# A hybrid decoder step: the state-space scan's states stored by step within the chunk, chunks innermost

## What is computed

```python
a = rmsnorm(h); z = a @ w_in               # q, k, v, o, gates and u
hm = mlstm_chunkwise(q, k, v, ig, lf, ...) # 4 heads of 256
bu = einsum('gpc,bsgc->bsgp', Bb, u)       # complex: bu_re, bu_im; 64 groups x 64 states, 16 channels each
bu[:, 0] += ab * s0                        # the state before, complex
st = associative_scan(st[t] = ab * st[t-1] + bu[t])      # complex, over the tokens
ys = einsum('gcp,bsgp->bsgc', C_re, st_re) - einsum(..., C_im, st_im) + Dd * u
ys = gelu(ys); ys = ys * sigmoid(ys @ w_glu + b_glu)
h = h + concat(hm, ys) @ w_out
h = h + peer_ffn(rmsnorm(h)); h = h + (p @ w_ple_proj) * sigmoid(rmsnorm(h) @ w_ple_gate)
```

## Time and profile before

| | us |
|---|---|
| median of 3 runs | 3019.16 |
| lowest, highest run | 3017.88, 3020.06 |
| span of the profiled execution, first to last instruction (its own time beside the span is not listed) | 3016.9 |
| TensorE busy in it | 2834.0 (94%) |
| VectorE busy | 1717.4 (57%) |
| ScalarE busy | 1213.0 (40%) |

### The profile page before, as it was taken

How to read it: one execution, slowest core, us unless ns; L and a number is a source line. 1 busy time by engine, 2 the same in 40 slices (tenths; PEclk the granted TensorE clock), 3 DMA queues, 4 the chain that set the end, 5 groups by cost and what they waited for, 6 DMA issues and landing times.

```text
span 3016.9 us, 53624 instructions
## 1 busy us (share of the span) xinstructions
PE 2834.0 (94%) x19564; PEld 2661.5 (88%) x19564; DVE 1717.4 (57%) x3311; ACT 1213.0 (40%) x2023; POOL 2.5 (0%) x18
## 2 busy tenths in 40 slices
PE   8999946899899998799999999999999999999997
PEld 6677734669799997699999999999999999999887
DVE  2289895566658887933333333335555555555466
ACT  1200002213344446944444444444444444444443
POOL 0000000000000000000000000000000000000000
PEclk9799977779899999999999999999999999999999
DMA  6124412226543331033333333344445544444543
GB/s 163 56 91 132 139 56 86 87 84 182 157 133 125 125 129 66 0 125 127 137 125 126 136 127 125 132 151 166 166 167 167 164 155 162 162 166 166 171 112 115
DMA packets 218075, 389.29 MB, mean 129 GB/s; under 512 B 21348, under 2 KB 167396, under 8 KB 200676
## 3 DMA queue, kind: packets, MB, share of 16 engines
q1 hardware_dynamic: 218020, 388.56, 39.0%
HBM read 374.04 MB, written 14.49 MB: 129 GB/s over the span
## 4 chain that ended last, share of the span: by engine, by line
PE 78%; DVE 14%; issue 4%; ACT 2%; DVEq 1%; DMA 0%; ACTq 0%
PE ps L389 11%; PE ps L390 11%; PE ps L391 11%; PE ps L1182 9%; PE ps L1185 9%; PE ps L1181 9%; PE ps L1113 7%; PE ps L261 3%; PE ps L812 1%; PE ps L1723 1%; DVE work L544 1%; DVE work L547 1%; DVE work L539 1%; DVE work L540 1%; DVE work L541 1%
## 5 line engine op out<-in xcount | busy, mean ns | idle before, releaser
L389 PE MATMUL ps<-ffn_h,part_h 128*128 128x288 f32 x2176 | 685.8, 315 | 14.8 <-issue 10.3
L390 PE MATMUL ps<-ffn_l,part_h 128*128 128x288 f32 x2176 | 642.3, 295 | 0.0
L391 PE MATMUL ps<-ffn_h,part_l 128*128 128x288 f32 x2176 | 639.1, 294 | 0.0
L1181 PE MATMUL ps<-act_h,v_high 128*128 128x288 f32 x2048 | 551.8, 295 | 6.1 <-DVE act_l L1418 3.6
L1182 PE MATMUL ps<-act_l,v_high 128*128 128x288 f32 x2048 | 552.2, 295 | 0.0
L1421 DVE TENSOR_TENSOR v_low<-ring,v_high 128x1024 fp32r<-128x1024 f32 x256 | 313.8, 1226 | 372.1 <-ACT v_high L1292 372.1
L1214 ACT CAST part_h<-ps 128x512 fp32r<-128x512 f32 x512 | 299.7, 586 | 466.1 <-PE ps L1113 465.4
L445 DVE TENSOR_TENSOR part_l<-ps,part_h 128x512 fp32r<-128x512 f32 x368 | 254.0, 691 | 404.9 <-ACT part_h L1214 402.4
L389 PEld LDWEIGHTS ps<-ffn_h,part_h 128*128 128x128 f32 x2176 | 409.8, 188 | 18.0 <-issue 16.2
L390 PEld LDWEIGHTS ps<-ffn_l,part_h 128*128 128x128 f32 x2176 | 412.0, 189 | 0.0
L391 PEld LDWEIGHTS ps<-ffn_h,part_l 128*128 128x128 f32 x2176 | 409.7, 188 | 0.0
(11 more groups left out here) (339 smaller groups left out, 3212.2 us busy)
## 6 DMA issues: line engine op xcount, KB each, us to landing
ring<-in_peer_u SPq DMA_DIRECT2D x128, 1024.0 KB, 5.3
ring<-in_peer_v SPq DMA_DIRECT2D x128, 1024.0 KB, 5.6
ring<-in_w_in SPq DMA_DIRECT2D x20, 2048.0 KB, 8.0
ring<-in_w_out SPq DMA_DIRECT2D x16, 1024.0 KB, 5.9
ring<-in_w_ple_gate SPq DMA_DIRECT2D x16, 1024.0 KB, 5.9
out<-work SPq DMA_DIRECT2D x37, 256.0 KB, 3.2
work<-in_state_mlstm_C SPq DMA_DIRECT2D x32, 256.0 KB, 4.9
ring<-in_peer_w_q SPq DMA_DIRECT2D x8, 1024.0 KB, 5.7
```

Source lines behind the costliest of these rows:

```text
L389: pe.matmul(bank, w_h, rhs_h, start=start, stop=False)
L390: pe.matmul(bank, w_h, rhs_l, start=False, stop=False)
L391: return pe.matmul(bank, w_l, rhs_h, start=False, stop=stop)
L1181: pe.matmul(ps[c][:, 0:T], w_h, a_h, start=st_, stop=False)
```

## The change

The states get two arrays for each part: `stp` for the prompt, indexed step, tile, chunk, and `sts` for the samples, indexed step, tile, request. What one step of the scan touches is then one dense piece: 512 elements for the prompt, 256 for the samples. The copies out of PSUM put the states in that order: each of the 2 x 32 copies becomes two instructions, one over 256 and one over 32 elements, that read PSUM with a step between neighbours. TensorE's y matmuls read the states from the two arrays, so each becomes two, of 256 and 32 columns, and their result is in the order of the arrays; VectorE's operation on it puts the tokens back in order, again in two instructions. The bytes, the arithmetic and the buffers' places are the same.

```diff
--- before.py
+++ after.py
@@ -176,11 +176,16 @@
                 ap = ap.rearrange("p (a b c) -> p a b c", b=shape[1], c=shape[2])
             return ap
 
+        def by_step(ap, n):
+
+            return ap.rearrange("p (c s) -> p s c", s=n)
+
         def bc(ap, n):
 
             return ap.unsqueeze(len(ap.shape)).to_broadcast([*ap.shape, n])
 
-        st = [wk(O_RE, NJ, T), wk(O_IM, NJ, T)]
+        stp = [wk(o, CH, NJ, NCH) for o in (O_RE, O_IM)]
+        sts = [wk(o + NJ * TP, NS, NJ, NB) for o in (O_RE, O_IM)]
         zT = wk(O_Z, 32, T)
         uT = wk(O_U, 8, T)
         mix = wk(O_MIX, 16, T)
@@ -572,22 +577,20 @@
             for _ in range(3):
                 cmul(v, o, pw, pw, pw, ts)
 
-            smp = [s[:, :, TP:T].rearrange("p j (b s) -> p s j b", s=NS) for s in st]
             s0 = [s0T[:, q, :].rearrange("p (b j) -> p j b", j=NJ) for q in range(2)]
             aB = [bc(x, NB) for x in a]
             for s in range(NS):
-                src = s0 if s == 0 else [x[:, s - 1] for x in smp]
-                cmul_add(v, o, [x[:, s] for x in smp], aB, src, [t[:, :, 0:NB] for t in tS])
-
-            chk = [s[:, :, 0:TP].rearrange("p j (k t) -> p t j k", t=CH) for s in st]
+                src = s0 if s == 0 else [x[:, s - 1] for x in sts]
+                cmul_add(v, o, [x[:, s] for x in sts], aB, src, [t[:, :, 0:NB] for t in tS])
+
             aC = [bc(x, NCH).unsqueeze(1) for x in a]
             tC = [t.unsqueeze(1) for t in tS]
             with v.Fori(0, CH - 1) as i:
                 o.loop(i, {"dve_own": CMUL})
-                cmul_add(v, o, [x[:, ds(i + 1, 1)] for x in chk], aC, [x[:, ds(i, 1)] for x in chk], tC)
+                cmul_add(v, o, [x[:, ds(i + 1, 1)] for x in stp], aC, [x[:, ds(i, 1)] for x in stp], tC)
                 o.leave(CH - 1)
 
-            end = [s[:, :, CH - 1:TP:CH] for s in st]
+            end = [x[:, CH - 1] for x in stp]
             with v.Fori(0, NCH - 1) as i:
                 o.loop(i, {"dve_own": CMUL})
                 cmul_add(v, o, [x[:, :, ds(i + 1, 1)] for x in end], [x.unsqueeze(2) for x in pw],
@@ -601,14 +604,14 @@
             prev = [x[:, :, 0:n].unsqueeze(1) for x in end]
             with v.Fori(0, CH - 1) as i:
                 o.loop(i, {"dve_own": CMUL + 6})
-                cmul_add(v, o, [x[:, ds(i, 1), :, 1:NCH] for x in chk], [bc(x, n).unsqueeze(1) for x in g2], prev,
+                cmul_add(v, o, [x[:, ds(i, 1), :, 1:NCH] for x in stp], [bc(x, n).unsqueeze(1) for x in g2], prev,
                          [t[:, :, 0:n].unsqueeze(1) for t in tS])
                 cmul(v, o, g2, g2, a, ts)
                 o.leave(CH - 1)
             for q in range(2):
-                o.do(v.tensor_copy(send[:, q, 0, :], st[q][:, :, TP - 1]))
+                o.do(v.tensor_copy(send[:, q, 0, :], end[q][:, :, NCH - 1]))
                 o.do(v.tensor_copy(send[:, q, 1:1 + NB, :],
-                                   st[q][:, :, TP + NS - 1:T:NS].rearrange("p j b -> p b j")))
+                                   sts[q][:, NS - 1].rearrange("p j b -> p b j")))
             o.settle()
             o.do(v.tensor_copy(g2[0], g2[0]), sem("s5_ready"))
             o.do(v.tensor_copy(g2[1], g2[1]), sem("send_ready"))
@@ -1731,9 +1734,10 @@
                 if u >= 2:
                     pe.wait_ge(sem("y_sum"), u - 1)
                 for r in range(4):
-                    for q in range(2):
-                        m = pe.matmul(ps[4 + u % 2][32 * r:32 * r + 32, 0:T], CT[q][:, u, 32 * r:32 * r + 32],
-                                      st[q][:, 4 * u + r, :], start=(q == 0), stop=(q == 1))
+                    for cols, x in ((slice(0, TP), stp), (slice(TP, T), sts)):
+                        for q in range(2):
+                            m = pe.matmul(ps[4 + u % 2][32 * r:32 * r + 32, cols], CT[q][:, u, 32 * r:32 * r + 32],
+                                          x[q][:, :, 4 * u + r, :], start=(q == 0), stop=(q == 1))
                 m.then_inc(sem("y_done"), 1)
 
             pe.wait_ge(sem("send_ready"), 1)
@@ -1813,7 +1817,9 @@
                               ps[4 + g % 4][:, 0:512].rearrange("p (a b) -> p a b", b=P)), sem("bct_copied"))
             for j in range(NJ):
                 act.wait_ge(sem("bu_done"), 2 * j + 1)
-                o.do(act.copy(st[0][:, j, :], ps[4 + 2 * (j % 2)][:, 0:T]), sem("bu_copied0"))
+                bu = ps[4 + 2 * (j % 2)]
+                o.do(act.copy(stp[0][:, :, j, :], by_step(bu[:, 0:TP], CH)))
+                o.do(act.copy(sts[0][:, :, j, :], by_step(bu[:, TP:T], NS)), sem("bu_copied0"))
             copy_tiles("z", zT)
 
             for u in range(8):
@@ -1868,13 +1874,18 @@
             dve_s5_setup(v, o)
             for j in range(NJ):
                 v.wait_ge(sem("bu_done"), 2 * j + 2)
-                o.do(v.tensor_copy(st[1][:, j, :], ps[5 + 2 * (j % 2)][:, 0:T]), sem("bu_copied1"))
+                bu = ps[5 + 2 * (j % 2)]
+                o.do(v.tensor_copy(stp[1][:, :, j, :], by_step(bu[:, 0:TP], CH)))
+                o.do(v.tensor_copy(sts[1][:, :, j, :], by_step(bu[:, TP:T], NS)), sem("bu_copied1"))
             v.wait_ge(sem("bu_copied0"), NJ)
             dve_s5_scan(v, o)
             for u in range(8):
                 v.wait_ge(sem("y_done"), u + 1)
-                o.do(v.scalar_tensor_tensor(uT[:, u, :], uT[:, u, :], gv[:, 80 + u:81 + u], ps[4 + u % 2][:, 0:T],
-                                            ALU.mult, ALU.add), sem("y_sum"))
+                for cols, n in ((slice(0, TP), CH), (slice(TP, T), NS)):
+                    y = ps[4 + u % 2][:, cols].rearrange("p (s c) -> p c s", s=n)
+                    uc = uT[:, u, cols].rearrange("p (c s) -> p c s", s=n)
+                    o.do(v.scalar_tensor_tensor(uc, uc, gv[:, 80 + u:81 + u], y, ALU.mult, ALU.add),
+                         None if n == CH else sem("y_sum"))
             dve_gate_rows(v, o)
             base = STREAM["glu"][0]
             for c in range(8):
```

## The result

The kernel with the change takes 2975.43 us, the median of four runs (2974.01 to 2978.06); the kernel before, on the same chip, 3018.52 (3017.54 to 3020.06). The ratio is 0.9856, with an interval of 0.9842 to 0.9870. It is 43 us faster, 16 us less than forecast, and outside the range.

What follows compares the result with a forecast made beforehand. The scan's end, then z's, was taken to bound the kernel. Scan -64.6, copies +1.5 and y on TensorE +2.9 sum to -60.2 us, taking 3019.2 to 2959 us, with a range of 2949 to 2971.

Steps and rivals of the forecast that it cites:

- What bounds the kernel: Before y, TensorE waits 64.6 us for the scan's end; gains there count only until z's end.
- The scan: VectorE's scan: dense operands instead of stepped ones save 87.6 us, of which 64.6 us can be used.
- partial cure: Scan on VectorE: dense layout saves under 64.6 us, so it still ends last; at half, 2981 us; chance 0.05.
- another cause: Scan on VectorE: something other than the step slows it, so only costs are left, 3025 us; chance 0.03.
- The copies: Copies out of PSUM, two instructions for one: +1.5 us, 0.1 us a period, as PSUM's step costs nothing.
- the reading against the change: Copies out of PSUM: the skill's 8-byte line rule, applied to copies, would make the sum some 3.6 us higher.
- y on TensorE: y stage on TensorE: 128 added short records cost 4.5 us, full-clock entry saves 1.6; 12.7 us in all, +2.9.
- Rival 2: y stage on TensorE: short matmuls and 64-byte pieces at their upper end, y 21 us, total 2967; chance 0.14.
- The 64-byte pieces: y matmuls on TensorE: reading the moving operand in 64-byte pieces costs nothing, at worst +4 us.
- What stands behind y: Stages after y: nothing else moves; same DMAs on the same waits, glu weights there in time.
- y on VectorE: VectorE's operation on y's result: two instructions, at most 0.48 + 0.25 us, hidden by TensorE; zero cost.
- The clock behind y: TensorE after y: clock doesn't fall, glu takes 31.1 us for 34.2, stretch before it 1.8 less; 2954; chance 0.12.

Runs made afterwards that it cites:

- The padded runs: e1_groups_in_turn with scan multiplications repeated: one more in the first loop, 2958.58 us; two more in both the first and third loops, 2972.85 us.
- e1_groups_in_turn: The changed kernel with, for each y tile, all four groups' 256-column matmuls first, then their 32-column ones: 2956.71 us, ratio 0.9795 to the kernel before.
- e4_short_first: The changed kernel with each group's 32-column y matmuls placed before its 256-column ones: 2956.01 us, ratio 0.9793 to the kernel before.

## Why the prediction was wrong, point by point

- **What bounds the kernel** was right: the scan's end, then z's. The padded runs show both sides of the limit; the surplus of 23 us was forecast and is what the trace has (387.2 to 410.4).
- **The scan** was right in its cause and size. Only the layout changed in these operations, and each shape went to the dense rate within 6 ns. The third loop still goes in 32 pieces of 15 elements and runs at the dense rate too, so it is the step between neighbours and not the number of pieces. The scan ends at 387.2 us; the forecast was 386.5 plus the copies' 1.5. The rivals of a partial cure and of another cause fall.
- **The copies** were right: +1.0 us at z's end for a forecast of 1.5. VectorE's copy of 256 elements takes 425 ns for the 423 worked out, so a step of 64 bytes in PSUM costs it nothing. The rule on PSUM lines of the Trainium skill's page "Advanced Engine Details and Errata", section Memory Cachelines, doesn't carry over to these reads: the 3.6 us of the reading against the change didn't come.
- **y on TensorE failed.** The step of the prediction read: the 128 short records cost 4.5 us, "9 if it doesn't scale, and 0 if these hide beside the other column groups, which already overlap: 16 records in 0.97 us". It priced the added matmuls as an addition to a stage whose overlap it took as given. The cost lay in the old ones: placing four more records of a group behind its first four took the overlap of the groups away, and 128 long records at 0.216 us in series are 27.6 us. Rival 2, y dearer, named the stage but the wrong mechanism and 21 us. By themselves the short matmuls cost about 2 us for the 4.5 of the sum (9.6 us in e1_groups_in_turn, 7.65 without them). The estimate from the page "TensorEngine Tiling (Array Packing)" of the Trainium skill, section Instruction Overhead, 6.4 us for the short ones, is above this 2 us and likewise far below the stage's 19. The same row that gave 0.97 us would have led to the right question: how can 16 records be through in the time of 4, if a group's stand together in the program? Something has to hold them, and it has a size.
- **The 64-byte pieces** of the moving operand were taken as free, and are: 0.216 us for 256 columns with them, and in the old layout too.
- **What stands behind y** was taken as unchanged. In the profiled executions it is 2535.8 us for 2533.1, 2.7 longer, with 159 us at half clock for 143; that is a part of the miss and not of the change's making as far as the runs show.
- **y on VectorE** was right in cost: two instructions take 0.64 us, and TensorE's own time hides them.
- **The clock behind y** (rival 1): it stayed full through y, but still fell in the broadcasts: the mean was 0.79 in the stretch before glu and 0.95 in glu, 0.74 and 0.91 before. The two stretches are 1.4 us shorter together (41.0 for 42.4), a part of the 5 us of that rival, and behind them it was at half for longer than before.

With y at e1's 9.6 us the sum would be -64.6 + 1.0 - 0.2 = -63.8, or 2955.4; e1_groups_in_turn measured 2956.7 and e4_short_first 2956.0.

## What to carry to other kernels

When an instruction of an overlapped stage is split in two, ask first what the overlap hangs on, and only then what the pieces cost: here the order of the same 256 records made 9.6 or 28.9 us. In matmuls that go to different groups of 32 output partitions, change the group after at most 4 records (two fp32 matmuls), or put the short ones first. And where a gain on one engine ends at another engine's end, as here at z, work out that cap before anything else; the layout gained 87 us on VectorE and 64 could be used.

## What the runs showed of the hardware that was not expected

- TensorE takes matmul records for one group of 32 output partitions ahead only up to 4, in the program's order. Groups of 4 records overlap fully (7.65 us for 128 records of 256 columns). A group with 6 lets the next one start after 0.461 us, one with 8 after 0.893 (four of 256 columns first), 0.52 (144 columns each) or about 0.15 (four of 32 columns first). Whether it is the records of a group or its weight loads that are counted, these runs don't tell apart: each record has one. Nor do they tell 4 records from 2 whole fp32 matmuls of two records, since every run has whole ones; both give the same starts.
- Neighbours 64 bytes apart in SBUF in one of the two operands (for the additions, done in place, in the result as well) slow VectorE's fp32 operations from 684 to 1023 ns for 512 elements (the multiplications) and from 692 to 1065 (the additions); 16 bytes apart from 424 to 626 ns for 256. In PSUM, 64 bytes apart cost VectorE's copy nothing.
